# Start of a streaming-encoder step: squares of x by token, h taken from the turned banks, copies on two engines, and the first norm in the third strip

## The chip, the cores and the metric

One core of one Trainium2 chip runs the whole program in one launch. The metric is the device time in microseconds of that launch. Engines are named as the profile names them: PE (TensorE matmul), PEld (its weight load), DVE (VectorE), ACT (ScalarE), POOL (GpSimd), SP (the queue that issues most DMAs).

## The reference, cut to what matters

One layer of an encoder runs on 256 prompt tokens and 32 sample tokens (288 columns together, D_MODEL 2048, D_FF 5504), all in float32:

```python
x = x + 0.5 * swiglu_ffn(x, g0, w_gate[0], w_up[0], w_down[0])
h = rmsnorm(x, g1); z = h @ w_in          # three groups of attention heads
x = x + concat(A, B, C) @ w_out
x = x + 0.5 * swiglu_ffn(x, g2, w_gate[1], w_up[1], w_down[1])
# rmsnorm(x, g) = x * rsqrt(mean(x*x) + 1e-6) * g
# swiglu_ffn    = (silu(h @ w_gate) * (h @ w_up)) @ w_down,  h = rmsnorm(x, g)
```

The change touches only the first norm and the first strips of the first feed-forward net, and the loading of small inputs and cached keys beside them.

## The kernel before, in words

x lives transposed in `xT` (128 features x 16 tiles x 288 tokens). Every product goes through a "strip": 128 output features, a stationary weight strip of 16 tiles of 128x128 (`raw`, 512 KB for each half of 8 tiles), and 288 moving columns. A weight and an activation are each split in a high part (fp32r) and a rest: ACT writes `w_hi` (L938), DVE writes `w_lo = raw - w_hi` (L1216), and PE does three matmuls per tile (hi.hi L510, lo.hi L511, hi.lo L512), 48 per strip. There are two buffers of everything for strips. The loops over strips (`bodies`, L318) run a gate strip and an up strip per turn; SP loads the strip after next as soon as its buffer has been split (`load`, L429).

The norm of x is applied late: the products are of `h = x * g`, and the evacuation multiplies by `rstd`, which is found from a sum of squares. So products can start before the sum is known.

The start before: SP issues x_sample, x_prompt in four column quarters (`load_x`, L398) with the halves of the first gate strip between them, the first up strip, and then the small inputs (L449 to L460). PE turns x tile by tile (`turn_x`, L724: two transposes of 128 rows and one of the 32 sample rows per tile, into five banks used in turn). The first 11 turns (`AHEAD`) stand before the first strip; the other five are issued inside it, one ahead of each of its first five tiles (`when`, L779). DVE copies each turned tile to `xT` (L1408), ACT makes `h_hi` from `xT` (`h_upper`, L948) and the square of `xT` (L1088), DVE makes `h_lo` (L1226), POOL adds up the squares (L1609). After its seventh tile (j == 6) ACT waits until both halves of the first strip have landed and splits them (L1090); DVE follows (L1419). After strip 0, PE does one matmul over `sumsq` (`x_norm`, L547), ACT takes the root (L955), DVE the reciprocal (L1235). After strip 1, PE turns the small inputs and the nine cached key tiles (`turn_others`, L732), a bank each, while DVE copies them out (`place_others`, L1421). Then the loop over the other strips begins.

What orders the work is each engine's own instruction stream and counting semaphores: `start_tr` (turned), `start_cp` (copied), `hlo_rdy` (h_lo of a tile), `hi_rdy` and `lo_rdy` (halves split), `used` (strip multiplied), `evac` (strip's result read), `acc_rdy` (sum of squares).

## Time and profile before

| | |
|---|---|
| median of 3 runs | 2146.34 us (2145.31 to 2147.26) |
| the profiled execution | 2145.73 us |
| its span | 2144.2 us |
| busy PE, PEld, DVE, ACT, POOL | 2123.4, 2073.5, 1178.2, 864.5, 96.0 us |

The span runs from the first to the last instruction; 1.5 us of the execution lie outside it. In a timeline row the first number is the start from the span's beginning, the second the time covered by the row's instructions, and brackets name the idle time before it and what ended it. A matmul's printed length includes its latency, so the distance from one start to the next says what one costs.

### The profile page before, as it was taken

What the parts mean: (1) busy time and instruction counts of PE and PEld (TensorE: products, weight loads), DVE (VectorE), ACT (ScalarE), POOL (GpSimd) and SP (SyncE); (2) the same over time, 40 slices, a digit from 0 to 9 for tenths busy, and PEclk for the clock granted to TensorE, in tenths of its full rate; (3) what the DMA queues carried; (4) which work ended last, traced back from release to release, by engine and by line L of the source; (5) the groups of instructions that cost most, each with busy time, mean ns of one, the idle gap of its engine ahead of it and who ended that gap; (6) DMA issues with size and microseconds to landing.
All of it is one profiled execution on the core that took longest, in us unless ns stands there. A gap on an engine that the chain in (4) does not pass through costs nothing. (4 is left out here: it accounts for less than half of the span.)

```text
span 2144.2 us, 42770 instructions
## 1 busy us (share of the span) xinstructions
PE 2123.4 (99%) x15935; PEld 2073.5 (97%) x15935; DVE 1178.2 (55%) x1807; ACT 864.5 (40%) x1347; POOL 96.0 (4%) x142
## 2 busy tenths in 40 slices
PE   8999999999999999999999999999999999999999
PEld 7999999999999999998887899999999999999999
DVE  6555444544445556588777765555444554455543
ACT  5333333333333344335557644333333333333333
POOL 3000000000000000022222100000000000000000
PEclk9999999999999999999999999999999999999999
DMA  6665666656656556555564356565665656656664
GB/s 191 169 163 156 167 166 161 171 158 167 165 158 171 160 155 178 150 149 135 134 139 102 100 170 171 160 171 156 166 169 160 171 156 167 169 157 169 160 170 132
DMA packets 681995, 339.88 MB, mean 159 GB/s; under 512 B 59203, under 2 KB 679085, under 8 KB 681880
## 3 DMA queue, kind: packets, MB, share of 16 engines
q1 hardware_dynamic: 673816, 329.38, 57.7%
q0 software_dynamic: 2944, 7.47, 1.5%
q10 hardware_dynamic: 5184, 2.39, 0.4%
q8 instruction: 28, 0.46, 0.1%
q14 instruction: 23, 0.19, 0.0%
HBM read 334.46 MB, written 5.30 MB: 158 GB/s over the span
## 5 line engine op out<-in xcount | busy, mean ns | idle before, releaser
L510 PE MATMUL bank<-h_hi,w_hi 128*128 128x288 f32 x3344 | 999.0, 299 | 0.4 <-issue 0.3
L511 PE MATMUL bank<-h_lo,w_hi 128*128 128x288 f32 x3344 | 988.1, 295 | 0.0
L512 PE MATMUL bank<-h_hi,w_lo 128*128 128x288 f32 x3344 | 984.9, 295 | 0.0
L1216 DVE TENSOR_TENSOR w_lo<-raw,w_hi 128x1024 fp32r<-128x1024 f32 (+2 forms) x642 | 740.0, 1191 | 264.8 <-ACT w_hi L938 264.1
L938 ACT ACTIVATE w_hi<-raw 128x1024 fp32r<-128x1024 f32 (+2 forms) x642 | 627.9, 1022 | 287.1 <-PE bank L512 262.9
L510 PEld LDWEIGHTS bank<-h_hi,w_hi 128*128 128x128 f32 x3344 | 628.1, 188 | 8.0 <-issue 6.7
L512 PEld LDWEIGHTS bank<-h_hi,w_lo 128*128 128x128 f32 x3344 | 631.3, 189 | 0.0
L511 PEld LDWEIGHTS bank<-h_lo,w_hi 128*128 128x128 f32 x3344 | 629.6, 188 | 0.2
L510 PE MATMUL bank<-gu_hi,w_hi 128*128 128x288 f32 x1376 | 408.1, 297 | 0.0
L511 PE MATMUL bank<-gu_lo,w_hi 128*128 128x288 f32 x1376 | 406.7, 296 | 0.0
L512 PE MATMUL bank<-gu_hi,w_lo 128*128 128x288 f32 x1376 | 406.5, 295 | 0.0
L511 PEld LDWEIGHTS bank<-gu_lo,w_hi 128*128 128x128 f32 x1376 | 259.6, 189 | 0.0
L512 PEld LDWEIGHTS bank<-gu_hi,w_lo 128*128 128x128 f32 x1376 | 259.6, 189 | 0.0
L510 PEld LDWEIGHTS bank<-gu_hi,w_hi 128*128 128x128 f32 x1376 | 259.4, 188 | 0.2
L1108 ACT ACTIVATE gu_hi<-gu 128x288 f32 (+1 forms) x86 | 38.2, 445 | 398.0 <-DVE gu L1456 398.0
L1105 ACT ACTIVATE g_sig<-g_act 128x288 f32<-128x288 f32 x86 | 38.3, 445 | 295.1 <-DVE g_act L1241 295.1
L1491 DVE SCALAR_TENSOR_TENSOR xT<-bank,xT 128x288 f32 (+1 forms) x96 | 43.9, 457 | 193.9 <-PE bank L512 193.7
L1241 DVE TENSOR_TENSOR u_act<-bank,rstd 128x288 f32<-128x288 f32 x86 | 39.3, 457 | 169.1 <-PE bank L512 169.1
L1241 DVE TENSOR_TENSOR g_act<-bank,rstd 128x288 f32<-128x288 f32 x86 | 39.4, 458 | 122.2 <-PE bank L512 122.1
L510 PE MATMUL bank<-o_hi,w_hi 128*128 128x288 f32 x256 | 76.3, 298 | 1.0 <-DVE o_lo L1333 1.0
L1459 DVE TENSOR_TENSOR gu_lo<-gu,gu_hi 128x288 f32 (+1 forms) x86 | 39.5, 459 | 68.3 <-ACT gu_hi L1108 68.3
L511 PE MATMUL bank<-o_lo,w_hi 128*128 128x288 f32 x256 | 75.6, 295 | 0.0
(205 smaller groups left out, 1052.9 us busy)
## 6 DMA issues: line engine op xcount, KB each, us to landing
raw<-in_w_ffn_gate SPq DMA_DIRECT2D x172, 512.0 KB, 5.1
raw<-in_w_ffn_up SPq DMA_DIRECT2D x172, 512.0 KB, 5.2
raw<-in_w_ffn_down SPq DMA_DIRECT2D x96, 512.0 KB, 4.0
raw<-in_w_in SPq DMA_DIRECT2D x74, 512.0 KB, 5.0
raw<-in_w_ffn_down SPq DMA_DIRECT2D x64, 384.0 KB, 4.6
raw<-in_w_ffn_down SPq DMA_DIRECT2D x32, 448.0 KB, 4.9
raw<-in_w_out SPq DMA_DIRECT2D x64, 96.0 KB, 2.6
raw<-in_w_out SPq DMA_DIRECT2D x32, 160.0 KB, 3.2
```

The costliest lines, as they stand in the source:

```text
L510: pe.matmul(out, w_hi[b][:, k, :], hi, start=(k == first_k), stop=False)
L511: pe.matmul(out, w_hi[b][:, k, :], lo, start=False, stop=False)
L512: mm = pe.matmul(out, w_lo[b][:, k, :], hi, start=False, stop=(k == last_k))
L938: act.activation(w_hi[b][:, k, :], raw[b][:, k, :], ACT.Copy).then_inc(hi_rdy, 1)
L1105: act.activation(g_sig[:, :], g_act[:, :], ACT.Silu).then_inc(sig_rdy, 1)
L1108: act.activation(gu_hi[:, j, :], gu[:, :], ACT.Copy).then_inc(guh_rdy, 1)
L1216: dve.tensor_tensor(w_lo[b][:, k, :], raw[b][:, k, :], w_hi[b][:, k, :].bitcast(F32), ALU.subtract)\
L1241: return dve.tensor_tensor(dst, bank_w[b][rows, cols], rstd[rows, cols], ALU.mult)
L1459: dve.tensor_tensor(gu_lo[:, j, :], gu[:, :], gu_hi[:, j, :].bitcast(F32), ALU.subtract).then_inc(gul_rdy, 1)
L1491: dve.scalar_tensor_tensor(dst, bank_w[buf(ph, s)][:, 0:NT], factor, xT[:, d, :], ALU.mult, ALU.add)\
```

## The change

ACT squares x by token in the layout in which it was loaded (`x_squares`: one instruction per 128 tokens, over 2048 columns, with a sum), takes two short roots (`x_deviation`), DVE takes two short reciprocals and scales the identity by them (`x_inverse`), and three matmuls against `mean_d` spread the result over the partitions. POOL no longer sums; it clears rows 32 to 127 of the sample block of `xrow` first. `h_hi` (ACT) and `h_lo` (DVE) are read from the turned bank instead of `xT`; the copy to `xT` is DVE's for even tiles and ACT's for odd ones. The first strip's halves are awaited and split singly, after tiles 5 and 9. The turns ahead of strip 0 are nine plain matmuls against the identity, the other seven (inside strip 0) transposes of three full blocks; nine 512-column matmuls on a constant tile stand at PE's very start, and sixteen of 288 columns after the ninth turn. The first pair's results are copied out raw (`first_pair`) and scaled later; the norm's matmul stands in the middle of the third strip. The cached key tiles are turned four to a bank. The two first turns of the strip loop are peeled.

```diff
...
+        warm = gu_hi[:, 0:2, :].rearrange("p k n -> p (k n)")[:, 0:512]
+        x_square = gu_lo[:, 0:8, :].rearrange("p k n -> p (k n)")[:, 0:D]
...
-                        for half, c in zip(pieces(ph, 0, 0), (2, 3)):
-                            load(ph, 0, 0, [half])
-                            load_x(c)
+                        halves = pieces(ph, 0, 0)
+                        load(ph, 0, 0, halves[:1], first_in)
+                        load_x(2)
+                        load(ph, 0, 0, halves[1:])
+                        load_x(3)
...
+                if index == 0:
+                    for rows, cols in ((P, slice(0, P)), (P, slice(P, T_P)), (T_S, slice(T_P, NT))):
+                        mm = pe.matmul(bank_m[:, cols], mean_d[0:rows, :], sumsq[0:rows, cols], start=True, stop=True)
+                    mm.then_inc(m_done, 1)
+                    return
...
             def start_slot(n):
-                if n >= len(bank_start):
-                    pe.wait_ge(start_cp, n - len(bank_start) + 1)
+                last = n - len(bank_start)
+                if last == 0:
+                    pe.wait_ge(start_cp, 1)
+                elif 0 < last < TURNED:
+                    pe.wait_ge(hlo_rdy, last)
                 return bank_start[n % len(bank_start)]
-            def turn_x(k):
+            def turn_x(k, plain):
+
                 b = start_slot(1 + k)
                 if k % 4 == 0:
                     pe.wait_ge(x_in[k // 4], 16)
-                for t in range(2):
-                    pe.transpose(b[:, t * P:(t + 1) * P], xrow[:, t, k * P:(k + 1) * P], ident[:, :])
-                pe.transpose(b[:, T_P:NT], xrow[0:T_S, 2, k * P:(k + 1) * P], ident[0:T_S, 0:T_S]).then_inc(start_tr, 1)
+                for t in range(3):
+                    src = xrow[:, t, k * P:(k + 1) * P]
+                    if plain:
+                        n = P if t < 2 else T_S
+                        mm = pe.matmul(b[:, t * P:t * P + n], src, ident[:, 0:n], start=True, stop=True)
+                    else:
+                        mm = pe.transpose(b[:, t * P:(t + 1) * P], src, ident[:, :])
+                mm.then_inc(start_tr, 1)
+
+            def keep_warm(count):
+                for _ in range(count):
+                    pe.matmul(bank_m[:, :], warm[:, 0:P], warm, start=True, stop=True)
...
-                for i, (src, _) in enumerate(CACHE_TILES):
-                    b = start_slot(TURNED + 3 + i)
-                    pe.transpose(b[:, 0:P], src, ident[:, :]).then_inc(start_tr, 1)
-
+                pe.transpose(b[:, 3 * P:4 * P], CACHE_TILES[8][0], ident[:, :]).then_inc(start_tr, 1)
+                for half in range(2):
+                    b = start_slot(TURNED + 3 + half)
+                    for i in range(4):
+                        mm = pe.transpose(b[:, i * P:(i + 1) * P], CACHE_TILES[4 * half + i][0], ident[:, :])
+                    mm.then_inc(start_tr, 1)
+
+            pe.wait_ge(warm_rdy, 1)
+            keep_warm(9)
...
-            AHEAD = 11
+            AHEAD = 9
+            pe.wait_ge(xs_padded, 2)
             pe.wait_ge(xs_in, 16)
             for k in range(AHEAD):
-                turn_x(k)
+                turn_x(k, True)
+            for i in range(16):
+                kind = i // 4
+                out = (bank_m, bank_w[1])[i % 2 if kind == 1 else 0]
+                rows = 64 if kind == 3 else P
+                moving = h_hi[:, 0, :] if kind == 2 else warm[:, 0:NT]
+                pe.matmul(out[0:rows, 0:NT], warm[:, 0:rows], moving, start=True, stop=True)
...
-                                turn_x(k + AHEAD)
+                                turn_x(k + AHEAD, False)
                             h_when(index)(k)
                         strip(ph, 0, 0, h_rhs, when)
-                        x_norm(index)
+                        if not begin:
+                            x_norm(index)
                         strip(ph, 0, 1, h_rhs)
                         if begin:
                             turn_others()
-                    with pe.Fori(1 if ph.more["first"] else 0, ph.strips // 2) as j:
+                            strip(ph, 1, 0, h_rhs, part=(0, 8))
+                            x_norm(index)
+                            strip(ph, 1, 0, h_rhs, part=(8, 16))
+                            strip(ph, 1, 1, h_rhs)
+                    with pe.Fori(2 if ph.n0 == 0 else 1 if ph.more["first"] else 0, ph.strips // 2) as j:
...
-            for j in range(DT):
-                act.wait_ge(start_cp, 2 + j)
-                h_upper(0, j)
-                if j >= 2:
-
-                    act.wait_ge(acc_rdy, j - 1)
-                act.activation((sqx, sd_x)[j % 2][:, :], xT[:, j, :], ACT.Square).then_inc(x_sq, 1)
-                if j == 6:
-                    split((phases[0], 0, 0))
+            def first_split(half):
+
+                act.wait_ge((first_in, ld[0])[half], 16)
+                act.activation(w_hi[0][:, 8 * half:8 * half + 8, :], raw[0][:, 8 * half:8 * half + 8, :], ACT.Copy).then_inc(hi_rdy, 1)
+
+            act.wait_ge(warm_rdy, 1)
+            act.activation(x_sd[:, :], warm[:, 0:3].bitcast(F32), ACT.Copy)
+            act.wait_ge(start_cp, 1)
+            for k in range(DT):
+                act.wait_ge(start_tr, 2 + k)
+                tile = bank_start[(1 + k) % len(bank_start)][:, 0:NT]
+                act.activation(h_hi[:, k, :], tile, ACT.Copy, scale=g_cols[:, k:k + 1]).then_inc(hhi_rdy, 1)
+                if copied_by_act(k):
+                    act.activation(xT[:, k, :], tile, ACT.Copy).then_inc(x_cp_act, 1)
+                if k in (5, 9):
+                    first_split(k // 9)
+
+            def x_squares(t):
+
+                rows = (P, P, T_S)[t]
+                if t:
+                    act.wait_ge(x_sq, t)
+                act.activation(x_square[0:rows, :], xrow[0:rows, t, :], ACT.Square, accum_out=x_ssq[0:rows, t:t + 1]).then_inc(x_sq, 1)
+
+            def x_deviation():
+                act.wait_ge(x_sq, 3)
+                act.activation(x_sd[:, 0:2], x_ssq[:, 0:2], ACT.Sqrt, bias=eps[:, :], scale=1.0 / D)
+                act.activation(x_sd[0:T_S, 2:3], x_ssq[0:T_S, 2:3], ACT.Sqrt, bias=eps[0:T_S, :], scale=1.0 / D).then_inc(x_sd_rdy, 1)
...
+                        if begin:
+                            x_squares(0)
+                            split((ph, 1, 0))
+                            x_squares(1)
+                            x_squares(2)
+                            x_deviation()
+                            split((ph, 1, 1))
+                            act.wait_ge(g_scaled, 1)
+                        elif ph.more["first"] and isinstance(j, int) and j == 0:
                             x_norm(2 * ph.more["ffn"])
                         act.wait_ge(evac, n + 1)
                         if not (isinstance(F, int) and F == 0):
                             act.wait_ge(gu_rdy, F)
                         act.activation(g_sig[:, :], g_act[:, :], ACT.Silu).then_inc(sig_rdy, 1)
-                        split(following(ph, j, 1))
+                        if not begin:
+                            split(following(ph, j, 1))
...
-            start_copy(1, xT[:, 0, :], slice(0, NT))
-            for j in range(DT):
-                if j + 1 < DT:
-                    start_copy(2 + j, xT[:, j + 1, :], slice(0, NT))
-                dve.wait_ge(start_cp, 2 + j)
-                h_tile(0, j, own_sum=False)
-                if j == 6:
-                    split((phases[0], 0, 0))
+            dve.wait_ge(start_cp, 1)
+            for k in range(DT):
+                tile = bank_start[(1 + k) % len(bank_start)][:, 0:NT]
+                dve.wait_ge(hhi_rdy, k + 1)
+                if copied_by_act(k):
+                    dve.wait_ge(x_cp_act, k // 2 + 1)
+                else:
+                    dve.tensor_copy(xT[:, k, :], tile)
+                dve.scalar_tensor_tensor(h_lo[:, k, :], tile, g_cols[:, k:k + 1], h_hi[:, k, :].bitcast(F32),
+                                         ALU.mult, ALU.subtract).then_inc(hlo_rdy, 1)
+                if k in (5, 9):
+                    split((phases[0], 0, 0), (k // 9,))
+
+            def x_inverse():
+
+                dve.wait_ge(x_sd_rdy, 1)
+                dve.reciprocal(x_inv[:, 0:2], x_sd[:, 0:2])
+                link(dve.reciprocal(x_inv[0:T_S, 2:3], x_sd[0:T_S, 2:3]))
+                for t, (rows, cols) in enumerate(((P, slice(0, P)), (P, slice(P, T_P)), (T_S, slice(T_P, NT)))):
+                    ins = dve.tensor_scalar(sumsq[0:rows, cols], ident[0:rows, 0:rows], x_inv[0:rows, t:t + 1], None, ALU.mult)
+                ins.then_inc(acc_rdy, DT)
+
+            def first_pair():
+
+                split((phases[0], 0, 1))
+                dve.wait_ge(used, 1)
+                dve.tensor_copy(sqx[:, :], bank_w[0][:, 0:NT]).then_inc(evac, 1)
+                split((phases[0], 1, 0))
+                dve.wait_ge(used, 2)
+                dve.tensor_copy(sd_x[:, :], bank_w[1][:, 0:NT]).then_inc(evac, 1)
+                place_others()
+                x_inverse()
+                split((phases[0], 1, 1))
+                dve.wait_ge(m_done, 1)
+                dve.tensor_scalar(rstd[:, :], bank_m[:, 0:NT], float(D), None, ALU.mult).then_inc(m_free, 1)
+                dve.wait_ge(m_free, 1)
+                dve.wait_ge(evac, 2)
+                dve.tensor_tensor(g_act[:, :], sqx[:, :], rstd[:, :], ALU.mult).then_inc(g_scaled, 1)
+                dve.tensor_tensor(u_act[:, :], sd_x[:, :], rstd[:, :], ALU.mult).then_inc(rstd_rdy, 1)
+                dve.wait_ge(rstd_rdy, 1)
             def place_others():
-                n = 1 + DT
+                n = TURNED
                 start_copy(n, qk_cols[:, :], slice(0, 6))
                 start_copy(n + 1, vec_t5[:, :], slice(0, VEC), slice(0, H_A + H_B))
-                start_copy(n + 2, vec_c[:, :], slice(0, VEC), slice(0, H_C))
-                for i, (_, dst) in enumerate(CACHE_TILES):
-                    start_copy(n + 3 + i, dst, slice(0, P))
+                start_copy(n + 2, vec_c[:, :], slice(0, VEC), slice(0, H_C), last=False)
+                start_copy(n + 2, kc_cache[:, 4, :], slice(3 * P, 4 * P))
+                for i in range(4):
+                    start_copy(n + 3, CACHE_TILES[i][1], slice(i * P, (i + 1) * P), last=i == 3)
+                start_copy(n + 4, kc_cache[:, 0:4, :].rearrange("p t c -> p (t c)"), slice(0, 4 * P))
...
-            for j in range(DT):
-                pool.wait_ge(x_sq, j + 1)
-                if j:
-                    pool.wait_ge(acc_rdy, j)
-                pool.tensor_tensor(sumsq[:, :], sumsq[:, :], (sqx, sd_x)[j % 2][:, :], ALU.add).then_inc(acc_rdy, 1)
-
+            pool.memset(xrow[T_S:2 * T_S, 2, :], 0.0).then_inc(xs_padded, 1)
+            pool.memset(xrow[2 * T_S:P, 2, :], 0.0).then_inc(xs_padded, 1)
+            pool.wait_ge(hlo_rdy, DT)
...
```

## Rows read from the trace of the kernel before

**Rows 1.** The page, part 1: busy time, share of the span, instructions.
```profile
PE 2123.4 (99%) x15935; PEld 2073.5 (97%) x15935; DVE 1178.2 (55%) x1807; ACT 864.5 (40%) x1347; POOL 96.0 (4%) x142
```

**Rows 2.** Who waited for whom, PE: total us, times, longest.
```profile
PE bank L729 <- DVE w_lo L1216: 0.9, 1, 0.9
```

**Rows 3.** Timeline of PE, start to the norm's matmul: start, us, engine, line, tile.
```profile
5.85 0.66 PE L729 MATMUL bank<-ident,xrow 128*128 128x128 f32 x2 [0.72 <-DMA xrow<-in_x_prompt]
...
7.55 0.69 PE L729 MATMUL bank<-ident,xrow 128*128 128x128 f32 x2
...
17.07 0.61 PE L510 MATMUL bank<-h_hi,w_hi 128*128 128x288 f32 x1
...
18.76 0.61 PE L510 MATMUL bank<-h_hi,w_hi 128*128 128x288 f32 x1
...
24.71 0.44 PE L510 MATMUL bank<-h_hi,w_hi 128*128 128x288 f32 x1
24.95 0.44 PE L511 MATMUL bank<-h_lo,w_hi 128*128 128x288 f32 x1
...
25.64 0.30 PE L511 MATMUL bank<-h_lo,w_hi 128*128 128x288 f32 x1
25.77 0.29 PE L512 MATMUL bank<-h_hi,w_lo 128*128 128x288 f32 x1
...
29.51 0.65 PE L550 MATMUL bank<-sumsq,mean_d 128*128 128x288 f32 x2
```

**Rows 4.** Busy time by stretch, with PE's granted clock after the engines.
```profile
20.00:25.00 5.00, 5.00 (x20) 3.91 (x19) 4.91 (x11) 4.39 (x11) 4.28 (x6) 1.00 0.88 270
```

**Rows 5.** Timeline of PE, end of strip 1 to strip 2.
```profile
36.24 0.29 PE L512 MATMUL bank<-h_hi,w_lo 128*128 128x288 f32 x1
...
37.37 0.82 PE L742 MATMUL bank<-flip,c_rows 128*10 128x128 f32 x6
38.12 0.44 PE L747 MATMUL bank<-ident,cache_rows 128*128 128x128 f32 x2
39.02 2.04 PE L747 MATMUL bank<-ident,cache_rows 128*128 128x128 f32 x7 [0.46 <-DVE qk_cols L1408]
41.02 0.40 PE L510 MATMUL bank<-h_hi,w_hi 128*128 128x288 f32 x1
```

**Rows 6.** Timeline of PE in the last stage, transposes between products.
```profile
2121.25 0.38 PE L763 MATMUL bank<-ident,y_t 128*128 128x128 f32 x2
...
2121.50 0.38 PE L510 MATMUL bank<-gu_hi,w_hi 128*128 128x288 f32 x1
```

**Rows 7.** DMA: issues in the timeline, and from issue to landing (KB, us).
```profile
2.42 0.47 SPq L435 DMA_DIRECT2D raw<-in_w_ffn_gate  x1
2.93 0.91 SPq L400 DMA_DIRECT2D xrow<-in_x_prompt  x1
...
20.31 1.19 SPq L435 DMA_DIRECT2D raw<-in_w_ffn_gate  x2
...
raw<-in_w_ffn_gate SPq DMA_DIRECT2D x1, 512.0 KB, 8.2
xrow<-in_x_prompt SPq DMA_DIRECT2D x1, 512.0 KB, 9.1
```

**Rows 8.** ACT, DVE and POOL in the start; one source line (min/median/max ns).
```profile
11.85 0.54 ACT L948 ACTIVATE h_hi<-xT,g_cols 128x288 fp32r<-128x288 f32 x1
12.29 0.43 ACT L1088 ACTIVATE sd_x<-xT 128x288 f32<-128x288 f32 x1
...
13.84 2.00 ACT L938 ACTIVATE w_hi<-raw 128x1024 fp32r<-128x1024 f32 x2 [0.15 <-DMA raw<-in_w_ffn_gate]
14.93 2.36 DVE L1216 TENSOR_TENSOR w_lo<-raw,w_hi 128x1024 fp32r<-128x1024 f32 x2 [0.57 <-ACT w_hi L938]
...
1.24 0.20 POOL L1591 MEMSET flip<- 128x128 f32 x1
...
L1226 DVE SCALAR_TENSOR_TENSOR h_lo<-xT,g_cols,h_hi x48: 503/519/827, 8.0 to 1310.5; - x26, 128x288 fp32r<-128x288 f32 x22
```

More of the change, by code:

```diff
@@ L320, in bodies @@
             count = ph.strips // strips
-            start = 1 if peel_first else 0
-            if peel_first:
-                body(0)
+            start = int(peel_first)
+            for j in range(start):
+                body(j)
             with eng.Fori(start, count - 1) as i:
@@ L427, in w_in_cols, with load @@
                 return [(r[:, :, c * HD:(c + 1) * HD], w[:, :, cols[c]]) for c in range(2)]
-            def load(ph, j, s, what=None):
+            def load(ph, j, s, what=None, landed=None):
                 n = strip_no(ph, j, s)
@@ L434, in load @@
                 for dst, src in what or pieces(ph, j, s):
-                    sp.dma_start(dst, src).then_inc(ld[buf(ph, s)], 16)
+                    sp.dma_start(dst, src).then_inc(landed or ld[buf(ph, s)], 16)
             for ph in phases:
@@ L1098, in body @@
                         n = strip_no(ph, j, 0)
-                        split(following(ph, j, 0))
-                        if ph.more["first"] and isinstance(j, int) and j == 0:
+                        begin = isinstance(n, int) and n == 0
+                        if not (isinstance(n, int) and n == 2):
+                            split(following(ph, j, 0))
+                        if begin:
[7 more added lines that the diff above has]
+                        elif ph.more["first"] and isinstance(j, int) and j == 0:
                             x_norm(2 * ph.more["ffn"])
@@ L1440, in body @@
                         later = not (isinstance(F, int) and F == 0)
[L1441 to L1450 removed]
+                        if isinstance(n, int) and n == 0:
+                            first_pair()
+                        else:
+                            if not (isinstance(n, int) and n == 2):
+                                split(following(ph, j, 0))
+                            if ph.more["first"] and isinstance(j, int) and j == 0:
+                                x_norm(2 * ph.more["ffn"], ph.n0)
+                            if later:
+                                dve.wait_ge(sig_rdy, F)
+                            read(n, buf(ph, 0), g_act[:, :]).then_inc(evac, 1)
+                            split(following(ph, j, 1))
+                            if later:
+                                dve.wait_ge(gu_rdy, F)
+                            read(n + 1, buf(ph, 1), u_act[:, :]).then_inc(evac, 1)
                         dve.wait_ge(evac, n + 2)
```

59 lines of the change are left out of this document (28 added, 31 removed).

## The prediction

> **What bounds the kernel now.** The page comes first: PE is busy 2123.4 of 2144.2 us [rows 1], and a steady strip is 48 matmuls 0.133 us apart, 6.4 us. The loops behind the first strips aren't touched, so the change can only move the moment from which PE runs without a break. That moment is read from PE's timeline. Strip 0 starts at 17.07 and the norm's matmul behind it at 29.51 [rows 3]; strip 1 ends at 36.37; the turns of the small inputs and cached keys fill the time to 41.02 [rows 5]. Strips 2 and 3 add 12.8: strip 3 ends at 53.8. The sum below asks when it ends after the change; everything later shifts with it.
>
> Two things make strip 0 slow: 12.4 us for 48 matmuls worth 6.4. Five turns of x stand in it, and PE runs at the lower of its two levels. Starts of 288-column products are 0.24 us apart at 24.71 and 0.13 apart at 25.64 [rows 3]: 288 columns at 1.2 GHz and at 2.4. The profile's granted clock doesn't show it (1.00 in every stretch, [rows 4]); the distances do. Until 17.07 PE did transposes only; the rate rose about 1 us after the last turn of x, 8.3 us after the first real product. The Trainium skill ("TensorE: Matmul & The Clock Gate", Part 4) says that transposes don't count as activity that raises the clock. By that rule, the trace agrees, and the nine plain matmuls per turn count where the transposes did not.
>
> Then the DMA. The first half of the first strip was issued at 2.42 and took 8.2 us: landed 10.6. The third quarter of x was issued at 2.93 and took 9.1: landed 12.0 [rows 7]. The second half is there at 13.84, where ACT stopped waiting for it [rows 8]. The order of these issues stays, so the landings do.
>
> **PE's chain after the change.** The warm matmuls start when DVE has set the tile, at about 1.7. Nine of 512 columns at the low level cost 512/288 x 0.24 = 0.43 each: until 5.5. They end before the first quarter of x is there (first turn at 5.85, [rows 3]), so they cost nothing. POOL's two clearings of 2048 columns: 0.20 us for 128 columns [rows 8], some 0.1 of it fixed, makes about 1.6 each, from 2.4 to 5.7. The bounds are 0.1 (a fixed cost alone) and 3.2 (all of it per column), so 2.6 to 8.8 for the pair's end; I take 5.7, nothing lost. Behind this wait stand all turns; 3 us would go straight to the first tile, but see the third quarter below.
>
 Before, a turn was 0.85 (5.85 to 7.55 is two, [rows 3]). Eight tiles: one or two low, the rest high, from 5.9 to 12.3. The ninth needs the third quarter of x (12.0), so up to here everything is hidden behind the DMA. It ends at 13.0.
>
> Sixteen filler matmuls of 288 columns: 16 x 0.133 = 2.1, on the path, until 15.1. Seven transposed turns and seven products: a turn among products at the high level is 0.25 to the next product plus a longer first start, 0.33 [rows 6]; with three blocks of full width I take 0.35, and a product tile is 0.40: 7 x 0.75 = 5.2, until 20.3. Nine more tiles at 0.40: 3.6. Strip 0 ends at 23.9. Strip 1 takes 6.4: 30.3.
>
> The small turns: the front part (36.37 to 38.12) stays 1.75. Nine transposes took 38.12 to 41.02, with 0.46 waited for a bank and then paced by DVE's copies [rows 5]. Four to a bank, and with banks freed by h_lo long ago, they run at about 0.12 each (two of them in 0.44 with latency): 1.1. So 2.85 where 4.65 stood: 33.15. Strips 2 and 3: 12.8. The norm's three matmuls between the halves of strip 2: 288 columns in four cycles, 0.5, as much as the one matmul before. Strip 3 ends at 46.5 instead of 53.8: 7.3 less.
>
> **What must keep up beside it.** ACT per two tiles: two h_hi at 0.44 from start to start and one copy of 0.43 [rows 8], from a bank now; DVE per two tiles: one copy at 0.37 and two h_lo. h_lo took 0.50 at least, 0.52 in the middle, and up to 0.83 with POOL working beside [rows 8]; POOL's sums are gone, so I take 0.45 in a row (bounds 0.35 and 0.8, for a bank as source isn't in the trace). That is 0.65 a tile for each, 0.7 with the handovers, under PE's 0.75 up to tile 15. A half's split is 1.0 on ACT and 1.2 on DVE [rows 8]. The first stands behind tile 5 (turned near 10.5; the half landed at 10.6, so the new single wait costs nothing, and behind it wait h_hi 6 and its followers): w_lo ready at 14, before 15.1. In the kernel before, PE waited 0.9 at this place [rows 2], which goes. The second stands behind tile 9, turned at 15.4: ACT 16.3 to 17.3, DVE to 18.6; PE wants it at 20.3 or later. Turn 15 needs the bank of tile 10, whose h_lo comes at 19.4, just when PE is there. h_lo of tile 15 is ready near 22.5; PE needs it at 23.5. Strip 1's first half is split on DVE at 23.6, PE wants it at 23.9. These are margins of half a microsecond to one, so DVE is the next bound: with none of PE's costs, strip 0 could not end before 22.8.
>
> Later: strip 2's load is issued at 20.3 and took 5.8 (landed 26.1, [rows 7] for the issue), its split is done by 30, and PE wants it at 33.1. The squares by token: 128x1024 took 1.0 on ACT [rows 8], so 2048 columns 2.0, three of them 6.1, around the split of strip 2; with 1.7 for loading the root's table and two short roots (my estimate; it lies in the cover below) ACT is done at 33.8. DVE's inverses and three scalings: 0.8, to 34.7. PE asks at 36.4. Cover of 1.7 us; were each square 0.6 longer, the norm would begin to stall strip 2. Behind it: split of strip 3, done about 37.5, wanted at 39.9. POOL's cache copies start at 22.9 instead of 26.5 and share the DMA engines with strip 2's load; that has 3 us to give. All these edits I cost at nothing.
>
> **The sum.** -7.3, which counts no bubble at the new handovers and a rate that rises early in the turns. I take 0.3 off for them: -7.0. On the execution profiled, 2145.7 - 7.0 = 2138.7; the median of the runs lies 0.6 higher, so 2139.3. This case's own range: if the rate rises only after all plain turns, they end at 5.9 + 9 x 1.1 = 15.8 and strip 0 at 26.7: -4.5, 2141.8. If fillers and turns hide better, DVE's bound: -8.5, 2137.8. Chance 0.72.
>
> **Rivals.** (a) The higher rate is lost, or not yet there, in the mixed part, seven turns between products. For it: before, the rate stayed low through the whole mixed stretch; one turn and one product there took 1.69 (17.07 to 18.76, [rows 3]). Against it: after the rise, 2.9 us of nothing but transposes (38.12 to 41.02) did not bring it down, the products of strip 2 go on at 0.13. Price: seven times 1.58 from 15.1 is 26.2, then 1 us more at the low level as before, then 7.7 tiles at 0.4: strip 0 ends at 30.2, strip 3 at 52.8, -1.0: 2145.3. Chance 0.15. The Trainium skill's sentence on transposes (same page and part) would speak for this case, if half of PE's time is too little; it gives no other price.
>
> (b) ACT and DVE, reading banks and handing over through semaphores twice per odd tile, set the pace at 0.95 a tile as before, the 0.54 of h_hi and the 0.43 of the square laid end to end [rows 8]. Then, from tile 9 at 15.4 with the split between, tile 15 is ready at 18.6 + 5.7 = 24.3 and strip 1's half at 25.5: strip 0's end and strip 1's start slip 1.6, -5.4, 2140.9. It stays faster; within the main case's range. Chance 0.05.
>
> (c) Slower. The warm matmuls and plain turns don't raise the rate at all, and it rises, as before, only about 1 us after the last transpose among products. Then the nine plain turns cost 1.1 each (to 15.8), the fillers 0.24 each (to 19.6), seven mixed tiles 1.6 each (to 30.8), and strip 0 ends at 30.8 + 1.0 + 3.1 = 34.9, strip 3 at 57.5: +3.7, 2150.0. The deciding point is the level at which the fillers run: at 0.133 this case is dead. For it: nothing in this trace shows that fp32 passes with a narrow result raise the rate. Against it: nine wide products at the very start, and products did raise it by 25.6. Chance 0.08.
>
> **How the numbers follow.** About 0.2% (4.3 us) is what a measurement of this kernel can tell from no change. The main case is below 2142.0 nearly throughout (0.70 of 0.72), (b) counts 0.04 as faster, (a) is within 0.2% but for 0.03, (c) is split evenly. Faster 0.77, same 0.19, slower 0.04. The range takes the main case from 2137.4 and reaches into (a) at 2145.3.
>
> **What would show it.** Starts 0.13 apart in the fillers by 13 (right) or 0.24 (c); turn and product together 0.75 in strip 0, or 1.6 (a); DVE's last h_lo before or after PE's tile 15 (b); no wait of PE for the norm in strip 2; the turns of the small inputs in 2.85 instead of 4.65; strip 3's end at 46.5. Wrong altogether if strips behind the fourth no longer follow at 6.4.

## The result: 6.4 us faster, as predicted, and the profile after

| | before | after |
|---|---|---|
| median (range, runs) | 2146.05 us (2145.31 to 2147.76, 7) | 2139.68 us (2137.27 to 2141.98, 7) |
| ratio | | 0.9969, 95% interval 0.996 to 0.9978 |
| profiled execution | 2145.73 us | 2138.5 us |
| start of strip 3's last product | 53.77 us | 46.47 us |

Predicted: 2139.3 us, and strip 3's end at 46.5. The last line of the table is the one by which most kernels below are compared. It is the 96th product of strips 2 and 3; behind it the code is the same up to the strip loop's end. In both kernels 2092.0 us lie between it and the end of the execution (2138.5 - 46.47 and 2145.73 - 53.77), so the whole difference of the two executions, 7.2 us, arises ahead of it.

The page of the kernel after, part 1, in the columns of [rows 1]:

```profile
PE 2121.6 (99%) x15991; PEld 2077.2 (97%) x15991; DVE 1172.9 (55%) x1803; ACT 866.3 (41%) x1347; POOL 83.1 (4%) x128
```

The timeline of PE in the kernel after (start, us covered, engine, line, tile), from the start to the norm, beside [rows 3] and [rows 5]:

```profile
1.70 4.21 PE L764 MATMUL bank<-gu_hi 128*128 128x512 f32 x9 [1.70 <-DVE gu_hi L1476]
...
6.18 6.68 PE L757 MATMUL bank<-ident,xrow 128*128 128x128 f32 x54
12.70 1.31 PE L800 MATMUL bank<-gu_hi 128*128 128x288 f32 x8
13.84 0.69 PE L800 MATMUL bank<-h_hi,gu_hi 128*128 128x288 f32 x4
...
14.89 0.49 PE L759 MATMUL bank<-ident,xrow 128*128 128x128 f32 x3
15.13 0.38 PE L529 MATMUL bank<-h_hi,w_hi 128*128 128x288 f32 x1
15.35 0.29 PE L530 MATMUL bank<-h_lo,w_hi 128*128 128x288 f32 x1
15.48 0.30 PE L531 MATMUL bank<-h_hi,w_lo 128*128 128x288 f32 x1
15.61 0.49 PE L759 MATMUL bank<-ident,xrow 128*128 128x128 f32 x3
...
30.13 0.22 PE L770 MATMUL bank<-ident,qk_rows 6*128 6x6 f32 x1
...
31.95 1.04 PE L782 MATMUL bank<-ident,cache_rows 128*128 128x128 f32 x8
32.75 0.38 PE L529 MATMUL bank<-h_hi,w_hi 128*128 128x288 f32 x1
36.02 0.95 PE L571 MATMUL bank<-sumsq,mean_d 128*128 128x128 f32 x6
36.90 0.41 PE L529 MATMUL bank<-h_hi,w_hi 128*128 128x288 f32 x1
```

Eight fillers take 1.14 us, 0.14 each (12.70 to 13.84); before, at 24.71, a product of the same width was 0.24 [rows 3]. So PE is at its higher level (2.4 GHz) when strip 0 begins. A turn and its product take 0.73 (14.89 to 15.61), where they took 1.69. The small turns run from 30.04 to 32.75. The norm's matmuls cost 0.88 and PE waits for nothing there.

The same stretch on ACT and DVE in the kernel after:

```profile
22.44 1.91 ACT L1154 ACTIVATE gu_lo<-xrow 128x2048 fp32r<-128x2048 f32 x1
...
27.15 2.01 ACT L988 ACTIVATE w_hi<-raw 128x1024 fp32r<-128x1024 f32 x2 [2.71 <-DMA raw<-in_w_ffn_gate]
29.07 1.89 ACT L1154 ACTIVATE gu_lo<-xrow 128x2048 fp32r<-128x2048 f32 x1
...
33.10 1.28 ACT L1158 ACT_TABLE_LOAD   x1
...
34.60 0.28 ACT L1159 ACTIVATE x_sd<-x_ssq,eps 32x1 f32<-32x1 f32 x1
```

```profile
12.67 1.23 DVE L1296 TENSOR_TENSOR w_lo<-raw,w_hi 128x1024 fp32r<-128x1024 f32 x1 [0.36 <-ACT w_hi L1135]
...
21.14 0.93 DVE L1499 SCALAR_TENSOR_TENSOR h_lo<-bank,g_cols,h_hi 128x288 fp32r<-128x288 f32 x2
...
35.22 0.62 DVE L1510 TENSOR_SCALAR sumsq<-ident,x_inv 128x128 f32<-128x128 f32 x3
```

ACT has done one of its three squares (128 of the 288 tokens) when it comes to strip 2's split and stands 2.71 us for that strip's load, with two squares still behind it. DVE's scaled identity is done at 35.84; PE asks at 36.02. The norm was hidden by 0.2 us.

### The profile page after: what moved, and what is told of

Its sections match the earlier page's. It is cut to its first block and busy times, and to the rows that moved or that the text cites. A ratio compares the mean times of both kernels' runs of the same rounds, so it can differ in the third digit from the quotient of the medians.

```text
span 2136.9 us, 42825 instructions
## 1 busy us (share of the span) xinstructions
PE 2121.6 (99%) x15991; PEld 2077.2 (97%) x15991; DVE 1172.9 (55%) x1803; ACT 866.3 (41%) x1347; POOL 83.1 (4%) x128
```

## The experiments

Open after the result: whether the warm matmuls and plain turns did raise PE's rate, as the prediction says; what the other parts are worth alone; and how near the hidden parts are to the path. Below, "S3" stands for the start of strip 3's last product in the profiled execution (46.47 after, 53.77 before). The medians come from different sets of runs, each with its own runs of the kernel before (their medians lie between 2145.7 and 2146.6 us); the ratio is always to those.

### Without the nine warm matmuls

```diff
-            keep_warm(9)
+            keep_warm(0)
```

> The changed kernel without the nine 512-column matmuls at PE's start; the sixteen fillers stay. Theory (real matmuls before the turns raise PE's rate early): the plain turns start at 6.2 as now but run at the low level, 1.3 a tile instead of 0.67, for three to five tiles, so the ninth ends near 15 to 16 instead of 12.7 and strip 3 ends 2 to 3.5 us later than 46.5: 2141.5 to 2143.5. Rival (the third quarter of x and the banks set the pace anyway, or the plain turns raise the rate on their own at once): strip 3 ends within 0.5 us of 46.5, 2139 to 2140.

Measured: 2140.07 us (2138.65 to 2144.21, 9 runs), ratio to before 0.9971 [0.9962, 0.9981]; S3 48.38. PE's timeline has the turns slower and the fillers fast all the same:

```profile
14.62 1.30 PE L800 MATMUL bank<-gu_hi 128*128 128x288 f32 x8
```

The ninth turn ended at 14.6 instead of 12.7: 1.9 us in this execution, 0.4 between the medians, whose ranges overlap. The rate rose anyway before strip 0, with nine narrow plain turns as nearly the only work. The warm matmuls aren't what carries the gain. Nor can the 1.9 us be put down to them: in two kernels below that have all nine (the second square ahead of the split, POOL busy) the ninth turn ended at 14.8 and 14.65. In windows of 1 us the traces of all three count 6 or 7 matmuls of the plain turns up to 11 us and 10 to 12 from there on; in the kernel after it is 10 to 12 from 7 us on.

### All turns as transposes

```diff
-                turn_x(k, True)
+                turn_x(k, False)
```

> The changed kernel with the nine turns ahead of strip 0 as transposes, too; warm matmuls and fillers stay. Theory (only plain matmuls hold the rate; by the Trainium skill, page TensorE: Matmul & The Clock Gate, Part 4, transposes don't count): the rate is low again or still when the fillers begin, they are 0.24 apart and cost 3.8 instead of 2.1, and part of the mixed stretch is slow: strip 3 ends 2 to 6 us later, 2141.5 to 2146. Rival (any work of PE holds it): transposes are shorter than plain turns, the third quarter of x gates the ninth turn at 11.6, strip 3 ends 0 to 0.6 earlier: 2139 to 2139.7.

Measured: 2138.85 us (2137.94 to 2141.37, 5), ratio 0.9964 [0.995, 0.9977]; S3 46.77. Timeline of PE:

```profile
6.18 1.53 PE L759 MATMUL bank<-ident,xrow 128*128 128x128 f32 x12 [0.32 <-POOL xrow L1721]
8.63 1.51 PE L759 MATMUL bank<-ident,xrow 128*128 128x128 f32 x12 [0.91 <-DMA xrow<-in_x_prompt]
12.11 0.52 PE L759 MATMUL bank<-ident,xrow 128*128 128x128 f32 x3 [1.98 <-DMA xrow<-in_x_prompt]
12.38 1.30 PE L800 MATMUL bank<-gu_hi 128*128 128x288 f32 x8
```

### None of the clock's matmuls

The change without warm matmuls, without fillers, and with all turns transposed (three full blocks each):

```diff
-            keep_warm(9)
+            keep_warm(0)
-                turn_x(k, True)
+                turn_x(k, False)
-            for i in range(16):
+            for i in range(0):
```

> The changed kernel with none of what was meant for PE's rate: no matmuls at the start, no fillers, all turns as transposes. Theory (the rate stays at the low level through the mixed stretch, as in the kernel before): turn and product 1.6 together, strip 0 ends near 29, strip 3 near 52, so the rest of the change alone is worth 1.5 to 2.2, nearly all of it from the small turns: 2144 to 2145. Rival (the products raise the rate soon after they begin, whatever stands between them): strip 3 ends before 48.5, 2138.5 to 2141.

Measured: 2138.27 us (2136.9 to 2141.88, 5), ratio 0.9961 [0.9947, 0.9974]; the profiled execution was the slowest of them, S3 49.96. Timeline of PE:

```profile
6.17 5.28 PE L759 MATMUL bank<-ident,xrow 128*128 128x128 f32 x24 [1.21 <-POOL xrow L1721]
11.74 0.52 PE L759 MATMUL bank<-ident,xrow 128*128 128x128 f32 x3 [0.28 <-DVE h_lo L1499]
13.37 0.55 PE L759 MATMUL bank<-ident,xrow 128*128 128x128 f32 x3 [1.12 <-DVE w_lo L1296]
13.68 0.38 PE L529 MATMUL bank<-h_hi,w_hi 128*128 128x288 f32 x1
13.89 0.29 PE L530 MATMUL bank<-h_lo,w_hi 128*128 128x288 f32 x1
14.02 0.29 PE L531 MATMUL bank<-h_hi,w_lo 128*128 128x288 f32 x1
...
37.97 1.30 PE L571 MATMUL bank<-sumsq,mean_d 128*128 128x128 f32 x6 [2.87 <-DVE sumsq L1510]
...
39.61 0.44 PE L530 MATMUL bank<-h_lo,w_hi 128*128 128x288 f32 x1
39.85 0.44 PE L531 MATMUL bank<-h_hi,w_lo 128*128 128x288 f32 x1
```

Up to 13.68 PE did transposes and nothing else, 0.22 apart at first, and the first products are 0.13 apart. Transposes alone raised the rate. The Trainium skill ("TensorE: Matmul & The Clock Gate", Part 4) says that a transpose doesn't count as busy time of the engine the way a product does; this run speaks against it as far as the rise of the rate goes, and the measurement decides. The norm's line shows a cost of being early. Strip 2's load had been issued at 19.91 and landed only at 29.2 here, ACT stood 6.23 us for it, and the norm came 2.87 us late. Behind that stop PE was at the lower level again: the norm's matmuls took 1.30 where they took 0.95, and the products behind them stood 0.24 apart until 41.8.

### The same with short sample turns

The kernel of the last section, but the sample block is turned as 32 rows, as before the change, in every tile:

```diff
-                        mm = pe.transpose(b[:, t * P:(t + 1) * P], src, ident[:, :])
+                        mm = pe.transpose(b[:, T_P:NT], xrow[0:T_S, 2, k * P:(k + 1) * P], ident[0:T_S, 0:T_S])
```

> The changed kernel with none of the matmuls meant for PE's rate and all turns as transposes, and the sample rows turned as before, as a block of 32 rows instead of one of 128 padded with zeros. Without padding left out this kernel ran its first products 0.13 apart at 13.7. Theory (it is the padding that lets transposes raise the rate: three full blocks 0.215 apart leave PE no idle time, while the 32-row block costs 0.3 of idle time in each turn of 0.86): the first products are 0.24 apart, turn and product 1.6 to 1.7, strip 0 ends at 27 to 30 instead of 22.3, strip 3 at 50 to 53: 2142.5 to 2145.5. Rival (the rate was up for another reason, for instance an accident of the moment): first products 0.13 apart, strip 3 ends as without it, 47 to 50, 2138 to 2140.

Measured: 2146.19 us (2145.65 to 2147.87, 11), ratio 1.0006 [0.9997, 1.0015]; S3 53.99. The whole gain is gone. Timeline of PE:

```profile
6.17 0.69 PE L759 MATMUL bank<-ident,xrow 128*128 128x128 f32 x2 [1.08 <-POOL xrow L1723]
6.79 0.31 PE L761 MATMUL bank<-ident,xrow 32*128 32x32 f32 x1
7.04 0.69 PE L759 MATMUL bank<-ident,xrow 128*128 128x128 f32 x2
...
15.36 0.61 PE L529 MATMUL bank<-h_hi,w_hi 128*128 128x288 f32 x1
15.77 0.44 PE L530 MATMUL bank<-h_lo,w_hi 128*128 128x288 f32 x1
16.01 0.44 PE L531 MATMUL bank<-h_hi,w_lo 128*128 128x288 f32 x1
```

A turn with a short block takes 0.87 (6.17 to 7.04); with three full blocks it took 0.66 (24 blocks in 5.28). The smaller block costs more, and with it in the stream the first products are 0.24 apart: the lower level (1.2 GHz). In this run the rate rose at 29.1 us, 3.6 behind the end of the last turn of x at 25.48. The small turns were as short as in the change (2.6 us); strip 0, with seven slow turns in it instead of five, and the norm's longer matmuls took that back. This pair settles what lets transposes raise the rate: between these two kernels only the padding differs, and it is worth 7.9 us in the medians (2146.19 - 2138.27), with ranges that don't touch. Why full blocks do it and short ones don't is not shown.

### The clock's matmuls in the kernel before

Before, with nine warm matmuls and its eleven turns ahead of strip 0 made plain (each 128, 128 and 32 rows); `turn_plain` is written out for them:

```diff
+            pe.wait_ge(warm_rdy, 1)
+            for _ in range(9):
+                pe.matmul(bank_m[:, :], warm[:, 0:P], warm, start=True, stop=True)
...
-                turn_x(k)
+                turn_plain(k)
```

> The kernel before with the rate's parts alone: nine matmuls of 512 columns at the start and its eleven turns ahead of strip 0 plain instead of transposed (no fillers). Theory (PE at the high level in strip 0, but DVE and ACT keep their pace of 0.97 a tile, the last h_lo comes near 25 as before and the split of strip 1 behind it near 27.5): strip 1 starts about 2.3 earlier than before, 2143 to 2144.3, so a third of the gain needs no other part. Rival (the rate isn't kept through the mixed stretch here): 0 to 0.5 less, 2145.6 to 2146.3. Other rival (PE alone is the limit): 4 less, 2142.

Measured: 2146.78 us (2145.37 to 2157.69, 11), ratio 1.0007 [0.9997, 1.0017]; S3 53.02. The rate was high in the mixed part (products 0.13 apart), with short blocks in it, but a turn and product took 0.99 there. Timeline of PE in the plain turns:

```profile
8.56 0.71 PE L731 MATMUL bank<-ident,xrow 128*128 128x128 f32 x4
9.20 0.40 PE L732 MATMUL bank<-ident,xrow 32*128 32x32 f32 x2
9.54 0.71 PE L731 MATMUL bank<-ident,xrow 128*128 128x128 f32 x4
```

PE is never idle between them, so 0.98 (8.56 to 9.54) is what a plain turn with a short block costs; a transposed one before cost 0.87, and the eleven ended at 17.34 instead of 15.3. In the mixed part a transposed turn with a short block took 0.49 (18.39 to 18.88) at the higher level, where one of three full blocks took 0.24 in the kernel after. DVE's pace was 0.98 a tile as well, and PE waited for it behind the mixed part. The waits of PE in this kernel (us in all, times, longest):

```profile
PE bank L757 <- DVE qk_cols L1422: 0.8, 1, 0.8
PE bank L512 <- DVE w_lo L1229: 0.7, 2, 0.4
...
PE bank L512 <- DVE h_lo L1239: 0.3, 1, 0.3
```

So the rate can also be raised by warm matmuls with plain turns, short blocks and all, and alone it brings 0.75 us in the profile and nothing in the medians. It needs other edits beside it. The trace names full blocks, a faster DVE and small turns that wait for no bank; what each is worth here was not tried.

### Without the fillers

```diff
-            for i in range(16):
+            for i in range(0):
```

> The changed kernel without the sixteen 288-column fillers after the ninth turn. Theory (the rate is up by 7 and half of PE's time in products keeps it up; the fillers only stand on PE's path): PE waits for the first half of the strip until 13.9, then DVE's pace binds (its last h_lo near 21, as it has 1.1 less to wait for tile 9), strip 3 ends 1.0 to 1.5 us earlier: 2138 to 2138.7. Rival (with the fillers gone the rate falls back in the mixed part, turn and product 1.6 instead of 0.73): strip 3 ends 2 to 6 us later, 2142 to 2146.

Measured: 2137.86 us (2137.1 to 2140.47, 5), ratio 0.9961 [0.9948, 0.9975]; S3 46.8. PE waited 1.06 for the first half's `w_lo` in place of 2.2 us of fillers, the rate held, and strip 0 ended at 22.5, 1.1 earlier. Strip 2's load did not move with it (issued at 20.69, 20.70 in the kernel after), and the gain was lost again at the norm (timeline of PE):

```profile
36.25 1.05 PE L571 MATMUL bank<-sumsq,mean_d 128*128 128x128 f32 x6 [1.24 <-DVE sumsq L1510]
```

The fillers are dead weight, but only 1 us of them can be had, and the norm takes it.

### Without the fillers, the second square ahead of the split

```diff
-                            split((ph, 1, 0))
                             x_squares(1)
+                            split((ph, 1, 0))
```

> The changed kernel without the fillers, and with ACT's square of the second 128 tokens ahead of the split of strip 2 instead of behind it. Theory (without fillers strip 2 begins 1.2 us earlier, and the gain was lost to a wait of 1.24 for the norm's sum, because ACT stood idle for 4.2 us on strip 2's load with two squares still to do): the square fills that idle time, the roots come about 1.9 earlier, PE doesn't wait for the norm, and strip 3 ends near 45.4 instead of 46.5: about 1.1 less than the changed kernel, 2136.8 to 2138.6. Rival (another input of the norm's step is late, DVE's copies of the small inputs): the wait stays above 0.5 and strip 3 ends at 46.0 or later.

Measured: 2139.45 us (2136.06 to 2142.32, 6), ratio 0.9967 [0.9955, 0.9979]; S3 47.48. The norm's wait is gone. But in this execution the plain turns were at the lower level until about 11 us and ended at 14.76, two microseconds later than in the kernel after with the same instructions (timeline of PE):

```profile
6.19 8.58 PE L757 MATMUL bank<-ident,xrow 128*128 128x128 f32 x54
```

So strip 2 began at 33.78 instead of 31.58 without fillers, and that delay alone is more than the 1.24 us that PE had waited: the run doesn't show what the edit is worth. From strip 0's first product to S3 this kernel took 31.31 us, the kernel after 31.34 and the one without fillers 32.83. What the run did show is the next bound: ACT's roots were done at 33.1, but DVE was copying the small inputs and came to the inverses at 35.44 only, so the rival had the right input. And it shows the spread of the moment at which the rate rises.

### Cached tiles four to a bank, in the kernel before

```diff
-                for i, (src, _) in enumerate(CACHE_TILES):
-                    b = start_slot(TURNED + 3 + i)
-                    pe.transpose(b[:, 0:P], src, ident[:, :]).then_inc(start_tr, 1)
+                pe.transpose(b[:, 3 * P:4 * P], CACHE_TILES[8][0], ident[:, :]).then_inc(start_tr, 1)
+                for half in range(2):
+                    b = start_slot(TURNED + 3 + half)
+                    for i in range(4):
+                        mm = pe.transpose(b[:, i * P:(i + 1) * P], CACHE_TILES[4 * half + i][0], ident[:, :])
+                    mm.then_inc(start_tr, 1)
```

> The kernel before with one part of the change alone: the cached key tiles turned four to a bank and copied out so. Theory: of the 4.65 us from strip 1's end to strip 2's start the wait for a bank (0.46) and DVE's pace go, leaving 2.9 to 3.2, so 1.4 to 1.8 less: 2144.3 to 2144.8. Rival (PE then waits at the first full banks for DVE's copies instead, since here DVE comes to the first copy only 2.3 us after strip 1's end): 0 to 0.5 less, 2145.6 to 2146.2.

Measured: 2144.45 us (2142.27 to 2148.36, 11), ratio 0.9989 [0.998, 0.9998]. From their first matmul to strip 2 the small turns took 2.62 (36.85 to 39.47) instead of 4.55 (36.47 to 41.02), with no wait for a bank; S3 52.21, that is -1.56, as strips 0 and 1 had ended 0.4 later in this execution. The part adds on its own, as the sum had it.

### Both halves awaited together

```diff
-                act.wait_ge((first_in, ld[0])[half], 16)
+                act.wait_ge(first_in, 16)
+                act.wait_ge(ld[0], 16)
```

> The changed kernel with one part undone: before the first half's split ACT waits for both halves of the first strip. Theory (the second half lands at 13.3, the first at 10.4; behind ACT's wait stand h_hi 6 and all later tiles, and DVE has only half a microsecond of margin): ACT and DVE run 1.7 later from tile 6 on, the first products start at 15.6 or later, the split of strip 1 comes 1.7 later, strip 1 starts 1.2 to 1.7 later and strip 3 ends as much later than it does after the same ninth turn: 2140.5 to 2141.5. Rival (fillers and PE's own chain cover it): less than 0.5.

Measured: 2138.94 us (2137.99 to 2142.03, 6), ratio 0.9969 [0.9957, 0.9981]; S3 47.58. ACT stood 2.14 us for the second half and PE 0.98 for `w_lo`; with the ninth turn as early as in the kernel after (12.62 and 12.70), strip 0 begins 1.1 later and so does S3. The single wait is worth that in the profiled executions; the medians don't show it.

### All copies by DVE

```diff
-            return k % 2 == 1
+            return False
```

> The changed kernel with one part undone: DVE makes all sixteen copies to xT. Theory (DVE has 8 x 0.37 = 3.0 more to do before the split of strip 1 and is the next bound behind PE): its last h_lo comes 1.5 to 2.5 later, turn 15 and the last products wait for it, strip 1 starts 1.5 to 2.5 later, and strip 3 ends 1.5 to 2.5 later: 2141 to 2142. Rival (DVE's time before the third quarter of x lands absorbs most of it): below 0.7.

Measured: 2138.36 us (2137.52 to 2140.42, 6), ratio 0.9967 [0.9955, 0.9979]; S3 46.96. The last `h_lo` ended at 22.87 instead of 22.07 and PE waited 0.5 for strip 1's `w_lo`. From strip 0's first product to S3 it took 32.03 instead of 31.34, so splitting the copies between two engines is worth about 0.7 us in the profiled executions; the medians don't show it.

### POOL busy beside DVE

Sixteen additions of 128x288 on scratch by POOL, one behind each `h_hi`:

```diff
+            for step in range(16):
+                pool.wait_ge(busy_rdy, step + 1)
+                pool.wait_ge(hhi_rdy, step + 1)
+                pool.tensor_tensor(busy[:, :], busy[:, :], busy[:, :], ALU.add).then_inc(busy_rdy, 1)
```

> The changed kernel with POOL kept as busy as before: sixteen additions of 128x288 on a scratch tile, one per tile of h_hi. Theory (two-input work of DVE from and to SBUF shares a port with POOL; by the Trainium skill, page SBUF State Buffer, that is an exclusive lock): h_lo now reads a bank and h_hi, one SBUF input only, so its length stays 0.52; the half splits (two SBUF inputs) grow from 1.23 to at most 2; strip 3 ends 0 to 0.6 later than 46.5. Rival (POOL's sums did cost, by h_lo): h_lo 0.68 as before, DVE's last one 1.5 or more later than 22.0 and strip 3 1 us later.

Measured: 2138.89 us (2137.08 to 2139.91, 4), ratio 0.9965 [0.995, 0.9979]; S3 48.41, because the rate rose near 11 us and the plain turns ended at 14.65; from strip 0's first product to S3 it took 31.32, as in the kernel after (31.34). DVE's `h_lo` by source line (min/median/max ns):

```profile
L1501 DVE SCALAR_TENSOR_TENSOR h_lo<-bank,g_cols,h_hi x16: 508/509/518, 8.7 to 23.5; 128x288 fp32r<-128x288 f32 x16
```

With POOL adding beside it, `h_lo` took 0.51 as without. In the kernel before the longest had been 0.827 [rows 8], so the prediction's reason ("POOL's sums are gone") is not needed with a bank as source. For an `h_lo` that reads `xT` no run was made, but two traces show that the sums cost it time: the more of a sum was left when it began, the longer it took. In the kernel before it took 0.68 with 0.36 us left (begun at 20.33, the sum from 19.86 to 20.69), 0.62 with 0.30 left (8.89, the sum from 8.30 to 9.19) and 0.50 when begun ahead of a sum (18.56 and 18.64); in the kernel before with the clock's matmuls it took 0.51 with 0.19 left (10.99, the sum from 10.35 to 11.18).

### The version that the runs point to

Transposed turns, warm matmuls kept, no fillers, the second square ahead of strip 2's split, and POOL's cache copies held back until strip 1's result is read:

```diff
-                turn_x(k, True)
+                turn_x(k, False)
-            for i in range(16):
+            for i in range(0):
-                            split((ph, 1, 0))
                             x_squares(1)
+                            split((ph, 1, 0))
-            pool.wait_ge(hlo_rdy, DT)
+            pool.wait_ge(evac, 2)
```

> A version meant to beat the changed kernel: all turns as transposes (shorter than plain ones at the low rate, so it doesn't matter when the rate rises), the nine matmuls at the start, no fillers, ACT's second square ahead of the split of strip 2, and POOL's copies of the caches after the first two strips are read instead of after the last h_lo. Theory: the ninth turn ends at 12.4, the mixed stretch starts at 13.7, strip 0 ends at 22.3, strip 2's load lands at 26 as it has the DMA engines alone, no wait for the norm, strip 3 ends at 45.0 (46.6 in the changed kernel): 2136.5 to 2138 and less spread than the changed kernel. Rival (strip 2's load is as late as 27 to 29 without POOL's copies, too, and the norm's sum comes after 34.5): a wait of 0.5 to 2 at the norm, strip 3 ends at 45.5 to 47.

Measured: 2137.87 us (2135.89 to 2138.49, 5), ratio 0.9964 [0.995, 0.9978]; S3 45.14, the earliest of all. The ninth turn began at 11.46 and ended at 11.98, and PE waited 0.46 for `w_lo` and 0.8 at the norm. Strip 2's load still landed at 27.15, 6.7 us after its issue at 20.44; it took 6.45 in the kernel after, with the copies beside it. So holding POOL's copies back shows no gain. The wait at the norm is DVE's here: the roots were done at 32.85, and DVE, which had split strip 2 from 28.24 and then copied the small inputs, reached the inverses at 33.66. In the profile it is 1.3 us ahead of the change. Its interval overlaps that of the change, so the medians don't prove it better; all five of its runs are below the change's median.

### What moves single executions

Behind S3 all kernels run the same code for the rest, yet not in the same time. The profiled time less S3 comes to 2091.9 to 2092.5 us in seven of the kernels (before and after among them), to 2090.4 to 2090.8 in five, 2093.0 in one and 2094.6 in one. PE's granted clock in two stretches sorts them. In stretches (us, PE busy, granted clock, DMA share, GB/s), the kernel after, then the one without warm matmuls, then the one with transposed turns and fillers:

```profile
880.00:900.00 20.00, 18.61 (x128) 0.91 0.39 99
1200.00:1220.00 20.00, 18.50 (x154) 1.00 0.22 63
```

```profile
880.00:900.00 20.00, 17.48 (x132) 1.00 0.48 124
1200.00:1220.00 20.00, 18.50 (x154) 1.00 0.21 61
```

```profile
880.00:900.00 20.00, 18.31 (x127) 0.91 0.38 99
1200.00:1220.00 20.00, 18.50 (x134) 0.83 0.19 55
```

The dip at 880 (0.91) goes with 1.5 us, the one at 1200 (0.83) with about 2.5; what causes them is open. The seven have the first alone, the 2093.0 (the second square ahead of the split) has the second alone, the five have neither (without warm matmuls, POOL busy, halves together, all copies by DVE, the last version), the 2094.6 has both. Together with the ninth turn, which ends up to 2 us later or earlier, this is the size of a kernel's spread, 4.7 us for the change. So S3 ranks the variants, within the 2 us by which its own start can move, and a median of five doesn't. Where only the moment of the rise differs, the distance from strip 0's first product to S3 takes it out: 31.34 us in the kernel after, 31.32 without warm matmuls, 31.32 with POOL busy.

## Why the prediction was right

**The path.** The sum held step by step (predicted, measured): turns end at 13.0, 12.70; fillers 2.1, 2.19; a mixed tile 0.75, 0.73; strip 0's end 23.9, 23.6; strip 1's end 30.3, 30.0; small turns 2.85, 2.71; strip 3's end 46.5, 46.6; the profiled execution 2138.7, 2138.5. That the last two agree to 0.2 us is partly luck: the prediction had the rate rise after one or two turns, as it did in this execution, but with the same instructions two others rose near 11 us and had S3 at 47.48 and 48.41. The median lay 1.2 us above the profiled execution, not 0.6.

**Why the rate rose.** Here half of the reason was wrong and the number right. The prediction reads from the kernel before that transposes don't raise the rate and that warm matmuls and plain turns would. The second half held: the rate rose in the plain turns of the kernel after, and with warm matmuls and plain turns in the kernel before. The first half did not. The trace of before fitted it, but it fitted another reading as well: its turns held a 32-row block each. The pair above shows it: full blocks turned back to back raised the rate without any help, the same turns with a short block did not. So the padding, which the prediction counts only as 1.6 us of POOL's time per clearing and as wider blocks in the mixed turns, is enough to keep the gain without the clock's matmuls. The warm matmuls with plain turns are a second way to the same high rate, and with both in the change neither is missed alone. Whether the change with them would keep its gain with short blocks was not tried; each of its turns among products would cost 0.49 instead of 0.24.

**Readings of the kernel before.** Its rate rose about 1.6 us behind the last turn of x (23.82 to 25.43), not about 1; rivals (a) and (c) count 1 us. And the prediction's "nine plain matmuls per turn" are nine warm matmuls and nine plain turns of three matmuls each.

**POOL's clearing** ended at 6.13 (5.7 predicted): 1.8 us each. It held the turns back 0.3 to 0.4 us, and as the ninth turn waits for the third quarter of x, little or nothing of it reached strip 0.

**ACT and DVE in strip 0.** The first `w_lo` was ready at 13.8 (14 predicted), the last `h_lo` at 22.07 (22.5): no wait of PE on either. `h_lo` took 0.43 in a row from a bank (0.45 taken).

**The norm's cover** was 0.2 us, not 1.7. Three terms make it. Strip 2's load took 6.45 us and landed at 27.15 instead of 26.1, which moved all that ACT does behind it by 1.05; a square with its sum was 2.1 instead of 2.0; PE asked at 36.02 instead of 36.4. The prediction's warning (a stall if squares were 0.6 longer) named the right weak place, and the kernels without fillers fell into it (1.24 and 2.87 us).

**The norm's matmuls** cost 0.88, where 0.5 was taken: three blocks in two passes each, with a longer first start. The cost shows nowhere because strip 0 and the small turns gave it back.

**The rivals.** (a) and (c) did not come: the rate held through the mixed part and over waits of up to 1.98 us. (b) is near: with all copies on DVE about 0.7 us is lost, and in the kernel before with the clock's matmuls both DVE's pace and PE's own, with short blocks, are 0.98 to 0.99 a tile.

## What to carry to other kernels

When an engine runs at a low rate and several things differ between that stretch and a fast one, the trace names none of them as the cause; add and remove each alone before building on one. Here a block of 32 rows among blocks of 128 made a turn longer than a full one did (0.87 against 0.66), and where nothing else raised the rate it stayed low, so padding an odd block can pay though its work is waste. And an edit that makes a stage end earlier should be followed to the next load: each microsecond won ahead of a DMA that doesn't move with it is taken from the cover of what waits behind that DMA.

## What the runs showed that was not expected

- Transposes of full blocks raise PE to its higher level. The level fell back behind a stop of 2.87 us in one run and did not behind stops of 1.24 and 1.98 us in two others.
- The moment of the rise isn't fixed: in six kernels whose PE instructions up to the ninth turn are the same it came before 5.4 us in one, between 6 and 8 in three and near 11 in two, and the ninth turn ended between 12.5 and 14.8. The profile's granted clock read 1.00 through all of it; only the distances between matmuls show it.
- Two short dips of the granted clock (0.91 at 880 to 900 us, 0.83 at 1200 to 1220 us) come and go between kernels with the same code there, and go with 1.5 and about 2.5 us.
- The load of strip 2 took 6.45 us in the change and 9.3 us (19.91 to 29.2) when issued 0.8 us earlier, in one execution each; why was not found.
